# Recurrence states as 64x64 blocks per head, two chunks alternating, conditioning blocks moved behind the output norm

## The chip, the cores and the metric

The kernel runs on one core of one Trainium2 chip. The metric is the device time of one execution in microseconds (us), and a kernel's time is the median of its runs. The engines are TensorE (PE in the rows; its weight loads are PEld), VectorE (DVE), ScalarE (ACT), GpSimd (POOL) and SyncE (SP), which here only starts the loads of weights.

## The reference, cut to what matters

Two blocks of a model over 256 tokens of width 1024. The change lies in the first one, in the RWKV-7 recurrence over 8 heads of 64 and in what stands around it:

```python
mod = jax.nn.silu(c) @ cond_w + cond_b            # 6 x 1024 columns: 12 blocks of 512
shift1, scale1, gate1, shift2, scale2, gate2 = jnp.split(mod, 6, axis=-1)
...
y_conv = jax.nn.silu(layer_norm(conv(u) + conv_b, conv_ln_g, conv_ln_b))
# per token t and head: S is a 64 x 64 state
#   S_t = S_{t-1} diag(w_t) - (S_{t-1} kk_t)(kk_t * a_t)^T + v_t k_t^T ;  y_t = S_t r_t
y_rw = rwkv7_scan(rh, heads(decay), kh, vh, kk, ah)
y_rw = layer_norm(y_rw, eps=GN_EPS).reshape(bsz, seq, RW_WIDTH) * rw_lnx_g + rw_lnx_b
y_rw = (y_rw + bonus.reshape(bsz, seq, RW_WIDTH)) * g
y1 = jnp.concatenate([y_conv, y_rw], axis=-1) @ w_out
x = layer_norm(ALPHA * x + gate1[:, None, :] * y1, ln1_g, ln1_b)
```

After it come a product-key expert layer (8 heads, 16 experts a token, whose rows of 1024 floats are gathered from memory) and the second block (mixer, cross attention, feed-forward).

## The kernel before, in words

The engines run programs written out by hand, which meet in semaphores. TensorE's results go to 8 banks of PSUM; the list `JOBS` names every result in TensorE's order and the engine that takes it out, `assign_banks` deals the banks in that order, and `begin(name)` makes TensorE wait until the bank's last result has been taken out (`was_emptied`). `computed(engine, name)` is the wait the other way.

The recurrence runs in 4 chunks of 64 tokens. Tile t of 128 tokens holds chunks 2t and 2t+1, one in either half of the 128 partitions; `half_of(e)` is such a half. When the triangular inverses are done (`inv_t`, in five levels), TensorE computes:

- `wu`: per head and chunk 64 columns each of two products with the inverse, taken out by ScalarE;
- `conv_mean`, `conv_var`: the mean over channels of the convolution and of its square, by `channel_mean`; before the first it waits for the convolution's last taps (VectorE, `conv_ready`);
- `rdw`, `y_local`: what a chunk's queries read from the state before it, and from the chunk itself;
- `psi`, `phi`: what a chunk adds to the state, and the matrix by which it changes it, for a pair of heads as one 128x128 block each, of which VectorE keeps the two 64x64 diagonal blocks by a mask (L2157, L2161); it adds the decay on phi's diagonal (L2165);
- `state` 1 and 2: the state after chunks 1 and 2, each from the one before it (128x128 blocks of a head pair, L1073), and `y_state`: the states read by `rdw` (L1084);
- `y_mean`, `y_var`: mean and variance over a head's 64 channels (`over_heads`, L895), and then `out1`, the product with w_out (L1105), whose first half (of the contraction) needs the convolution's output, `y_conv_ready`, and whose second half needs the normalised recurrence, `mix_ready`.

Between these stand the conditioning vector's last blocks 8 to 11. `mod_parts(i)` (L810) multiplies silu(c) with a 1024x512 block of cond_w, which a load of 2 MB brings into one of four slots of `weight_ring`; VectorE adds bias and parts (`mod_bias`, L1973, into the single buffer `mod_sum`), `modulation(i)` (L816) sums over partitions, and ScalarE writes the result. `weight_blocks` lists the loads in order with slot and the job after which the slot is free; SyncE starts each when that job is done.

A float32 matmul has two records in the trace, one for each pass of the moving operand, so the 8 matmuls of a `by_head` half show as 16.

## Time and profile before

| | us |
|---|---|
| median of 3 runs (lowest, highest) | 1452.13 (1446.63, 1464.97) |
| profiled execution | 1464.34 |
| its span, first to last instruction | 1462.5 |
| PE / DVE / ACT / POOL busy in the span | 1168.3 / 890.2 / 507.3 / 574.2 |
| mean granted TensorE clock, share of full | 0.89 |
| first `wu` matmul, last `wu` matmul issued, first `out1` matmul | 178.8, 182.2, 234.3 |
| expert layer (gathers), about | 300 to 1073 |

The profile's times count from the span's start. An engine's busy time counts the records of its instructions; where TensorE's are short, a record covers more than the time by which the next one follows. The granted clock is a share of 2.4 GHz, and takes the two values 1 and 0.5 in this trace; a window's value is their mean.

### The profile page before, as it was taken

What the parts mean: (1) busy time and instruction counts of PE and PEld (TensorE: products, weight loads), DVE (VectorE), ACT (ScalarE), POOL (GpSimd) and SP (SyncE); (2) the same over time, 40 slices, a digit from 0 to 9 for tenths busy, and PEclk for the clock granted to TensorE, in tenths of its full rate; (3) what the DMA queues carried; (4) which work ended last, traced back from release to release, by engine and by line L of the source; (5) the groups of instructions that cost most, each with busy time, mean ns of one, the idle gap of its engine ahead of it and who ended that gap; (6) DMA issues with size and microseconds to landing.
All of it is one profiled execution on the core that took longest, in us unless ns stands there. A gap on an engine that the chain in (4) does not pass through costs nothing.

```text
span 1462.5 us, 17535 instructions
## 1 busy us (share of the span) xinstructions
PE 1168.3 (80%) x6306; PEld 769.8 (53%) x6306; DVE 890.2 (61%) x1704; ACT 507.3 (35%) x1098; POOL 574.2 (39%) x642
## 2 busy tenths in 40 slices
PE   4999989857988657587879487558749987799997
PEld 1977754744553223232354133223329966699985
DVE  3577745862545573767494585557475665488773
ACT  1564311314241322224133233123125543265551
POOL 5055300244546666576656666666610020000000
PEclk9999988978999888797879788768979998899999
DMA  9363543497989999899989999999975415256530
GB/s 355 119 237 116 176 144 112 149 355 276 334 327 386 338 378 377 334 381 335 383 306 340 350 368 365 378 335 375 365 285 194 144 34 168 72 185 193 185 137 30
DMA packets 139775, 381.11 MB, mean 261 GB/s; under 512 B 10708, under 2 KB 37743, under 8 KB 139707
## 3 DMA queue, kind: packets, MB, share of 16 engines
q0 software_dynamic: 73728, 268.47, 48.9%
q1 hardware_dynamic: 64656, 108.87, 21.7%
q10 hardware_dynamic: 1322, 2.85, 0.6%
q8 instruction: 45, 0.74, 0.2%
q14 instruction: 24, 0.19, 0.0%
HBM read 379.10 MB, written 1.05 MB: 260 GB/s over the span
## 4 chain that ended last, share of the span: by engine, by line
PE 51%; POOL 14%; issue 12%; DVE 10%; DMA 7%; ACT 3%; another core or an unknown queue 1%; DVEq 1%; ACTq 0%; SPq 0%; POOLq 0%
PE banks L1165 12%; POOL arena L731 8%; PE banks L841 7%; PE banks L843 7%; PE banks L842 7%; POOL arena L738 6%; PE banks L783 4%; PE banks L1124 3%; DMA arena<-in_peer_v,arena 3%; DMA arena<-in_peer_u,arena 3%; DVE arena L2303 2%; PE banks L955 2%; DMA weight_ring<-in_cond_w 2%; PE banks L1105 1%; PE banks L810 1%
## 5 line engine op out<-in xcount | busy, mean ns | idle before, releaser
L1165 PE MATMUL banks<-arena 128*128 128x512 f32 x1012 | 496.5, 654 | 186.3 <-issue 117.0
L1165 PEld LDWEIGHTS banks<-arena 128*128 128x128 f32 x1012 | 211.2, 212 | 468.8 <-issue 410.5
L2303 DVE SCALAR_TENSOR_TENSOR arena<-arena,banks 128x1024 f32<-128x1024 f32 x256 | 308.7, 1220 | 213.4 <-DMA arena<-in_peer_u,arena 173.1
L738 POOL DMA_INDIRECT arena<-in_peer_v,arena x256 | 243.6, 952 | 205.6 <-PE banks L1165 105.9
L731 POOL DMA_INDIRECT arena<-in_peer_u,arena x256 | 243.4, 951 | 80.7 <-issue 74.7
L843 PE MATMUL banks<-hi_h,low_slot 128*128 128x256 f32 (+2 forms) x600 | 171.4, 286 | 0.0
L1671 ACT ACTIVATE arena<-arena 128x8 f32<-128x8 f32 x32 | 6.7, 208 | 356.7 <-issue 182.8
L843 PEld LDWEIGHTS banks<-hi_h,low_slot 128*128 128x128 f32 (+2 forms) x600 | 113.0, 188 | 0.5
L841 PE MATMUL banks<-hi_h,hi_w 128*128 128x256 f32 (+1 forms) x352 | 101.3, 288 | 2.7 <-DVE lo_h L2408 2.7
L842 PE MATMUL banks<-lo_h,hi_w 128*128 128x256 f32 (+1 forms) x352 | 100.0, 284 | 0.0
L1666 ACT ACTIVATE arena<-ident,arena 128x128 f32<-128x128 f32 x256 | 78.3, 388 | 4.8 <-issue 4.2
L1677 ACT ACTIVATE arena<-arena 128x128 f32<-128x128 f32 x256 | 78.2, 388 | 3.4 <-issue 0.2
L1124 PE MATMUL banks<-hT,weight_ring 128*128 128x128 f32 (+1 forms) x384 | 62.0, 318 | 16.8 <-issue 15.2
L696 POOL TENSOR_TENSOR arena<-arena 128x512 f32<-128x512 f32 x30 | 43.0, 1434 | 74.0 <-ACT arena L1537 72.5
L841 PEld LDWEIGHTS banks<-hi_h,hi_w 128*128 128x128 f32 (+1 forms) x352 | 67.3, 191 | 3.1 <-DVE hT L2387 3.1
L1124 PEld LDWEIGHTS banks<-hT,weight_ring 128*128 128x128 f32 x384 | 56.3, 199 | 23.4 <-issue 18.3
L842 PEld LDWEIGHTS banks<-lo_h,hi_w 128*128 128x128 f32 (+1 forms) x352 | 67.3, 191 | 0.0
L2568 DVE SCALAR_TENSOR_TENSOR arena<-banks,col,arena 128x255 f32<-128x255 f32 (+3 forms) x88 | 38.4, 477 | 31.5 <-ACT arena L1906 30.8
L719 POOL COPY arena<-arena 128x16 uint32<-128x16 uint32 x16 | 3.4, 213 | 125.7 <-DVE arena L2283 125.6
L750 POOL TENSOR_TENSOR low_slot<-weight_ring,hi_out 128x4096 fp32r<-128x4096 f32 x1 | 8.9, 8903 | 109.7 <-ACT hi_out L1828 109.7
L783 PE MATMUL banks<-hT,weight_ring 128*128 128x256 f32 x192 | 49.1, 421 | 1.5 <-DVE hT L2387 0.8
L2419 DVE TENSOR_TENSOR low_slot<-weight_ring,hi_w 128x2048 fp32r<-128x2048 f32 (+1 forms) x22 | 49.2, 2242 | 1.8
(376 smaller groups left out, 1920.6 us busy)
## 6 DMA issues: line engine op xcount, KB each, us to landing
weight_ring<-in_cond_w SPq DMA_DIRECT2D x12, 2048.0 KB, 8.9
weight_ring<-in_w_in SPq DMA_DIRECT2D x11, 2048.0 KB, 9.0
weight_ring<-in_ffn_w_up SPq DMA_DIRECT2D x20, 1024.0 KB, 7.3
weight_ring<-in_ffn_w_down SPq DMA_DIRECT2D x5, 2048.0 KB, 7.8
weight_ring<-in_w_out SPq DMA_DIRECT2D x4, 2048.0 KB, 8.0
weight_ring<-in_peer_wq SPq DMA_DIRECT2D x4, 2048.0 KB, 8.0
arena<-in_peer_u,arena POOLq DMA_INDIRECT x256
arena<-in_peer_v,arena POOLq DMA_INDIRECT x256
```

The source lines that it names most:

```text
L731: g.indirect_dma_start(u_rows[:, j, :], None, A["peer_u"], bass.IndirectOffsetOnAxis(ap=row, axis=0)).then_inc(sem(f"u_in_{j}"), 16)
L738: g.indirect_dma_start(v_rows[:, j, :], None, A["peer_v"], bass.IndirectOffsetOnAxis(ap=row, axis=0)).then_inc(sem(f"v_in_{j}"), 16)
L783: last = mm(b[0:width, i * SEQ:(i + 1) * SEQ], w[:, k, f * P:f * P + width], src[:, k, :], start=(k == 0), stop=(k == KD - 1))
L841: mm(out_, sh, mh, start=first, stop=False)
L842: mm(out_, sh, ml, start=False, stop=False)
L843: return mm(out_, sl, mh, start=False, stop=last)
L1124: last = mm(b[:, half * n:half * n + n], w[:, k, f * P:f * P + P], hT[:, k, tok], start=(k == 0), stop=(k == KD - 1))
L1165: last = mm(acc[i], diag[:, r, j, :], v_rows[:, j, i * 512:(i + 1) * 512], start=False, stop=False)
L1666: fn(gate_diag[:, j, :], ident[:, :], ACT.Copy, scale=gates[:, bass.ds(n * TOPK + (8 * r + j), 1)])
L1677: ins = fn(diag[:, r, j, :], gate_diag[:, j, :], ACT.Copy, scale=gz[:, r, j:j + 1])
L2303: ins = v.scalar_tensor_tensor(out=u_rows[:, j, :], in0=u_rows[:, j, :], scalar=1.0, in1=h2_banks[t], op0=ALU.mult, op1=ALU.mult, accum_ou ...
L2419: signal(v.tensor_tensor(dst, w, hi_w[:, i % 4, :, 0:n], ALU.subtract), sem("up_split"))
```

## The change

1. `psi`, `phi` and `state` are computed per head as 64x64 blocks, two heads of a pair stacked on the two halves of the partitions; the masks go. VectorE writes decay times identity into phi early (two instructions before the convolution's taps of the first level) and later only adds phi's product.
2. Where two chunks of a tile are computed, their matmuls alternate (`state_in(0, 1)`, `read_matrix`, `own_chunk`), each chunk in its bank.
3. New order: psi, phi, states, rdw and y_local come right behind `wu`, ahead of `conv_mean`. ScalarE instead of VectorE takes psi out.
4. Conditioning blocks: `mod_parts(8)` stands behind `y_state`, `conv_var` and `y_mean` follow, `modulation(8)` stands between `y_mean` and `y_var`, and blocks 9 to 11 come behind `y_var`, ahead of `out1`. w_out's first half is loaded into the slot that block 9 leaves, ahead of the keys.
5. ScalarE takes `y_var` out ahead of the convolution's Silu; VectorE's reciprocal for `y_rs` stands behind `mod_bias(11)`.

```diff
@@ -115,19 +115,13 @@
...
+JOBS += [(("y_mean", i), "dve") for i in range(2)] + modulation_jobs(8) + [(("y_var", i), "act") for i in range(2)]
+JOBS += part_jobs(9) + part_jobs(10) + modulation_jobs(9) + part_jobs(11) + modulation_jobs(10) + modulation_jobs(11)
...
@@ -242,11 +236,11 @@
...
-              (("cond", 10), 3, ("modp", 10)), (("cond", 11), 2, ("modp", 11)), (("keys",), 1, ("keys_T", 3)),
-              (("w_out", 0), 3, ("out1", 0, 0)), (("w_out", 1), 2, ("out1", 1, 1)),
+              (("cond", 10), 3, ("modp", 10)), (("cond", 11), 2, ("modp", 11)),
+              (("w_out", 0), 1, ("out1", 0, 0)), (("keys",), 3, ("keys_T", 3)), (("w_out", 1), 2, ("out1", 1, 1)),
...
@@ -1022,56 +1016,79 @@
...
+            def state_in(*chunks):
+
+                banks = {c: begin("psi", c) for c in chunks}
+                for h in range(NHEAD):
+                    out_ = half_of(h % 2), slice(HD * (h // 2), HD * (h // 2) + HD)
+                    ch = slice(h * HD, (h + 1) * HD)
+                    for c in chunks:
+                        t, s = c // 2, half_of(c % 2)
+                        mm(banks[c][out_], kend_t[s, t, ch], v_t[s, t, ch], start=True, stop=False)
+                    for c in chunks:
+                        t, s = c // 2, half_of(c % 2)
+                        last = mm(banks[c][out_], bend_t[s, t, ch], wu[s, t, 1, h, :], start=False, stop=True)
+                        if h == NHEAD - 1:
+                            done(last)
+
+            def state_change(c):
+                b, t, s = begin("phi", c), c // 2, half_of(c % 2)
+                for h in range(NHEAD):
+                    last = mm(b[half_of(h % 2), HD * (h // 2):HD * (h // 2) + HD], wu[s, t, 0, h, :], bend_t[s, t, h * HD:(h + 1) * HD],
+                              start=True, stop=True)
+                done(last)
+
+            def read_matrix(t):
+                banks = [begin("rdw", t, e) for e in range(2)]
+                for h in range(NHEAD):
+                    for e in range(2):
+                        s = half_of(e)
+                        last = mm(banks[e][half_of(h % 2), half_of(h // 2)], wu[s, t, 0, h, :], pairs[s, t, PLACE[h], 1, :], start=True, stop=True)
+                        if h == NHEAD - 1:
+                            done(last)
+
+            def own_chunk(t):
+                banks = [begin("y_local", t, e) for e in range(2)]
+                for j in range(NPAIR):
+                    for h in (2 * j, 2 * j + 1):
+                        for e in range(2):
+                            s = half_of(e)
+                            mm(banks[e][half_of(h % 2), half_of(j)], v_t[s, t, h * HD:(h + 1) * HD], pairs[s, t, PLACE[h], 3, :],
+                               start=True, stop=False)
+                    for h in (2 * j, 2 * j + 1):
+                        for e in range(2):
+                            s = half_of(e)
+                            last = mm(banks[e][half_of(h % 2), half_of(j)], wu[s, t, 1, h, :], pairs[s, t, PLACE[h], 1, :],
+                                      start=False, stop=True)
+                            if h == NHEAD - 1:
+                                done(last)
...
                 b = begin("state", c)
                 if c == 1:
-                    pe.wait_ge(sem("phi_ready"), 2)
+                    was_emptied(pe, "psi", 0)
+                    was_emptied(pe, "phi", 1)
                 else:
                     was_emptied(pe, "state", 1)
                 src = psi[:, 0, :, :] if c == 1 else state[:, 0, :, :]
-                for j in range(NPAIR):
-                    last = mm(b[:, j * P:(j + 1) * P], phi[:, c - 1, j, :], src[:, j, :], start=True, stop=True)
+                for h in range(NHEAD):
+                    s, j = half_of(h % 2), h // 2
+                    last = mm(b[s, j * HD:(j + 1) * HD], phi[s, c - 1, j, :], src[s, j, :], start=True, stop=True)
                 done(last)
+
+            was_emptied(pe, "wu", 0, 1)
+            state_in(0, 1)
+            state_change(1)
+            read_matrix(0)
+            was_emptied(pe, "wu", 1, 1)
+            state_in(2)
+            state_change(2)
+            next_state(1)
+            read_matrix(1)
+            own_chunk(0)
+            next_state(2)
+            own_chunk(1)
+            channel_mean("conv_mean", conv, "conv_ready")
@@ -1080,16 +1097,24 @@
...
-                    for j in range(NPAIR):
-                        last = mm(b[:, j * P + half:j * P + half + CHUNK], src[:, j, :], rdw[:, t, j, half:half + CHUNK],
+                    for h in range(NHEAD):
+                        s, j = half_of(h % 2), h // 2
+                        last = mm(b[s, j * P + half:j * P + half + CHUNK], src[s, j, :], rdw[s, t, j, half:half + CHUNK],
                                   start=True, stop=True)
                 done(last)
-            mod_parts(11)
+            mod_parts(8)
+            channel_mean("conv_var", conv_t, "conv_sq_ready")
             was_emptied(pe, "y_state", 1)
             over_heads("y_mean", mean_head, y_rw)
-            modulation(11)
+            modulation(8)
             pe.wait_ge(sem("y_sq_ready"), 1)
             over_heads("y_var", mean_head, y_sq)
+            mod_parts(9)
+            mod_parts(10)
+            modulation(9)
+            mod_parts(11)
+            modulation(10)
+            modulation(11)
@@ -1597,36 +1622,43 @@
...
+            def take_psi(c):
+                computed(act, "psi", c)
+                empty(fn(psi[:, c, :, :], bank("psi", c)[:, 0:NPAIR * HD].rearrange("p (a b) -> p a b", b=HD), ACT.Copy), "psi", c)
+
+            def take_local(t):
                 for e in range(2):
                     computed(act, "y_local", t, e)
                     empty(fn(y_rw[:, :, (2 * t + e) * CHUNK:(2 * t + e + 1) * CHUNK],
                              bank("y_local", t, e)[:, 0:NPAIR * CHUNK].rearrange("p (a b) -> p a b", b=CHUNK), ACT.Copy), "y_local", t, e)
-                modulation(8 + t)
-                if t == 0:
-                    was_emptied(act, "conv_mean")
-                    signal(fn(conv_t, conv, ACT.Square), sem("conv_sq_ready"))
-                    computed(act, "conv_var")
-                    empty(fn(conv_r, bank("conv_var")[:, 0:SEQ], ACT.Sqrt, bias=eps[:, 0:1]), "conv_var")
-            modulation(10)
+
+            for c in range(NCH - 1):
+                take_psi(c)
+            act.wait_ge(sem("taps_added"), CONV_K - 1)
+            for t in range(NT):
+                take_local(t)
+            was_emptied(act, "conv_mean")
+            signal(fn(conv_t, conv, ACT.Square), sem("conv_sq_ready"))
+            computed(act, "conv_var")
+            empty(fn(conv_r, bank("conv_var")[:, 0:SEQ], ACT.Sqrt, bias=eps[:, 0:1]), "conv_var")
+            was_emptied(act, "y_mean", 1)
+            signal(fn(y_sq, y_rw, ACT.Square), sem("y_sq_ready"))
+            modulation(8)
+            for i in range(2):
+                computed(act, "y_var", i)
+                empty(fn(y_rs[:, 2 * i:2 * i + 2, :], bank("y_var", i).rearrange("p (a b) -> p a b", a=2), ACT.Sqrt,
+                         bias=eps[:, 1:2]), "y_var", i)
+            modulation(9)
...
@@ -2127,6 +2159,10 @@
...
+            was_emptied(dve, "rw_T", "bend", 1)
+            for c in (1, 2):
+                step(v.tensor_tensor(phi[:, c - 1, :, :], ident_c.unsqueeze(1).to_broadcast([P, NPAIR, HD]),
+                                     chunk_decay[:, :, c:c + 1].to_broadcast([P, NPAIR, HD]), ALU.mult))
@@ -2141,40 +2177,33 @@
...
+            def add_change(c):
+                computed(dve, "phi", c)
+                empty(v.tensor_tensor(phi[:, c - 1, :, :], phi[:, c - 1, :, :],
+                                      bank("phi", c)[:, 0:NPAIR * HD].rearrange("p (a b) -> p a b", b=HD), ALU.add), "phi", c)
+
+            def add_read(t):
                 for e in range(2):
                     computed(dve, "rdw", t, e)
                     empty(v.tensor_tensor(rdw[:, t, :, e * CHUNK:(e + 1) * CHUNK],
                                           bank("rdw", t, e)[:, 0:NPAIR * CHUNK].rearrange("p (a b) -> p a b", b=CHUNK),
                                           kr[:, :, t, 1, e * CHUNK:(e + 1) * CHUNK], ALU.add), "rdw", t, e)
...
+
+            def add_state(c):
                 computed(dve, "state", c)
-                empty(v.tensor_tensor(state[:, c - 1, :, :], bank("state", c).rearrange("p (a b) -> p a b", b=P), psi[:, c, :, :], ALU.add),
-                      "state", c)
+                was_emptied(dve, "psi", c)
+                empty(v.tensor_tensor(state[:, c - 1, :, :], bank("state", c)[:, 0:NPAIR * HD].rearrange("p (a b) -> p a b", b=HD),
+                                      psi[:, c, :, :], ALU.add), "state", c)
+
+            add_change(1)
+            add_read(0)
+            add_change(2)
+            add_state(1)
+            add_read(1)
+            add_state(2)
+            computed(dve, "conv_mean")
+            empty(v.tensor_tensor(conv, conv, bank("conv_mean")[:, 0:SEQ].unsqueeze(1).to_broadcast([P, 4, SEQ]), ALU.subtract),
+                  "conv_mean")
@@ -2182,12 +2211,17 @@
...
-            mod_bias(11)
+            mod_bias(8)
             for i in range(2):
                 computed(dve, "y_mean", i)
                 y = y_rw[:, 2 * i:2 * i + 2, :]
                 empty(v.tensor_tensor(y, y, bank("y_mean", i).rearrange("p (a b) -> p a b", a=2), ALU.subtract), "y_mean", i)
+            was_emptied(dve, "conv_var")
+            step(v.reciprocal(conv_r, conv_r))
+            settled()
+            signal(v.tensor_tensor(conv, conv, conv_r.unsqueeze(1).to_broadcast([P, 4, SEQ]), ALU.mult), sem("conv_n_ready"))
+            for i in (9, 10, 11):
+                mod_bias(i)
```

TensorE, from the last products with a mask to come to the first conditioning block, before (`L816` is modulation(8), `L1049` and `L1050` psi, `L1057` phi, `L918` conv_var, `L810` mod_parts(9)):

```order
L1049 MATMUL banks<-arena 128x128
L1050 MATMUL banks<-arena 128x128
L1057 MATMUL banks<-arena 128x128 [waits emptied_by_dve]
L1057 MATMUL banks<-arena 128x128 x3
L918 MATMUL banks<-arena,mean_all 128x256 [waits conv_sq_ready,emptied_by_dve]
L918 MATMUL banks<-arena,mean_all 128x256 x3
L810 MATMUL banks<-weight_ring,mem_kv 32x512 [waits slot_in_1,emptied_by_dve]
L810 MATMUL banks<-weight_ring,mem_kv 32x512 x7
```

The same engine now, where chunk 2's psi (L1027, L1030) ends and phi (L1037), state 1 (L1076), rdw of tile 1 (L1046) and y_local of tile 0 (L1056) follow:

```order
L1027 MATMUL banks<-arena 64x64
L1030 MATMUL banks<-arena 64x64
L1037 MATMUL banks<-arena 64x64 [waits emptied_by_act]
L1037 MATMUL banks<-arena 64x64 x7
L1076 MATMUL banks<-arena 64x64 [waits emptied_by_dve,emptied_by_act]
L1076 MATMUL banks<-arena 64x64 x7
L1046 MATMUL banks<-arena 64x64 [waits emptied_by_dve,emptied_by_act]
L1046 MATMUL banks<-arena 64x64 x15
L1056 MATMUL banks<-arena 64x64 [waits emptied_by_dve]
```

No mean, no conditioning block stands between them any more, and state 1 comes before the second tile's rdw and y_local.

TensorE from state 1 on, before (`L1073` state, `L1084` y_state, `L895` y_mean):

```order
L1073 MATMUL banks<-arena 128x128 [waits phi_ready,emptied_by_dve]
L1073 MATMUL banks<-arena 128x128 x3
L816 MATMUL banks<-mem_kv,ones 128x512 [waits emptied_by_dve]
L1073 MATMUL banks<-arena 128x128 [waits emptied_by_dve,emptied_by_act]
L1073 MATMUL banks<-arena 128x128 x3
L1084 MATMUL banks<-arena 128x64 [waits emptied_by_dve,emptied_by_act]
L1084 MATMUL banks<-arena 128x64 x3
L1084 MATMUL banks<-arena 128x64 [waits emptied_by_dve,emptied_by_act]
L1084 MATMUL banks<-arena 128x64 x7
L810 MATMUL banks<-weight_ring,mem_kv 32x512 [waits slot_in_2,emptied_by_dve]
L810 MATMUL banks<-weight_ring,mem_kv 32x512 x7
L895 MATMUL banks<-arena,mean_head 128x512 [waits emptied_by_dve] x2
```

The same engine now, from conv_mean (L912) on; `L1102` is y_state, `L804` mod_parts(8), `L889` y_mean and y_var, `L810` modulation(8):

```order
L912 MATMUL banks<-arena,mean_all 128x256 [waits taps_added,conv_ready,emptied_by_dve]
L912 MATMUL banks<-arena,mean_all 128x256 x3
L1102 MATMUL banks<-arena 64x64 [waits emptied_by_dve]
L1102 MATMUL banks<-arena 64x64 x7
L1102 MATMUL banks<-arena 64x64 [waits emptied_by_dve,emptied_by_act]
L1102 MATMUL banks<-arena 64x64 x15
L804 MATMUL banks<-weight_ring,mem_kv 32x512 [waits slot_in_2,conv_ready]
L804 MATMUL banks<-weight_ring,mem_kv 32x512 x7
L912 MATMUL banks<-arena,mean_all 128x256 [waits conv_sq_ready,emptied_by_act]
L912 MATMUL banks<-arena,mean_all 128x256 x3
L889 MATMUL banks<-arena,mean_head 128x512 [waits emptied_by_dve]
L889 MATMUL banks<-arena,mean_head 128x512 [waits emptied_by_act]
```

modulation(10) and mod_parts(11) have left the place around the states; blocks 9, 10 and 11 stand behind y_var now.

ScalarE between its last y_local (`L1604`) and y_var (`L1628`), before:

```order
L1522 ACTIVATE weight_ring<-banks,eps 128x512 [waits mm_done]
L1522 ACTIVATE weight_ring<-banks 128x512 [waits mm_done]
L1616 ACT_TABLE_LOAD
L1616 ACTIVATE hT<-arena,col 128x256 [waits conv_n_ready]
L1616 ACTIVATE hT<-arena,col 128x256 x3
L1622 DMA arena<-in_ln_g 128x1024 [waits y_conv_ready,mm_done]
L1622 DMA arena<-in_ln_b 128x1024
L1624 ACTIVATE arena<-arena 128x1024 [waits emptied_by_dve]
L1522 ACTIVATE weight_ring<-banks 128x512 [waits mm_done]
L1628 ACT_TABLE_LOAD
L1628 ACTIVATE arena<-banks,eps 128x512 [waits mm_done] x2
```

and now, from conv's square (L1641) to the last modulation (L1547):

```order
L1641 ACTIVATE arena<-arena 128x1024 [waits emptied_by_dve]
L1643 ACTIVATE arena<-banks,eps 128x256 [waits mm_done]
L1645 ACTIVATE arena<-arena 128x1024 [waits emptied_by_dve]
L1547 ACTIVATE weight_ring<-banks,eps 128x512 [waits mm_done]
L1649 ACTIVATE arena<-banks,eps 128x512 [waits mm_done] x2
L1547 ACTIVATE weight_ring<-banks,eps 128x512 [waits mm_done]
L1655 ACT_TABLE_LOAD
L1655 ACTIVATE hT<-arena,col 128x256 [waits conv_n_ready]
L1655 ACTIVATE hT<-arena,col 128x256 x3
L1659 DMA arena<-in_ln_g 128x1024 [waits y_conv_ready]
L1659 DMA arena<-in_ln_b 128x1024
L1547 ACTIVATE weight_ring<-banks 128x512 [waits mm_done] x2
```

y_var (L1649) is taken out ahead of the Silu (L1655), and the Silu, which `out1` waits for, stands behind modulation(9).

## Rows read from the trace of the kernel before

**Rows 1.** Windows of the stretch: busy us and records by engine, granted clock, DMA share.

```profile
182.50:185.90 3.40, 0.00 (x0) 0.00 (x0) 3.24 (x8) 0.60 (x1) 0.00 (x0) 0.81 0.00 0
185.90:192.40 6.50, 6.46 (x26) 3.15 (x26) 1.22 (x1) 0.00 (x0) 0.00 (x0) 0.57 0.00 0
...
212.30:216.00 3.70, 1.13 (x9) 1.00 (x9) 3.67 (x4) 0.00 (x0) 0.00 (x0) 0.91 0.67 214
216.00:228.40 12.40, 12.40 (x51) 8.28 (x51) 2.25 (x4) 3.95 (x6) 0.00 (x0) 0.50 0.45 167
...
234.30:262.00 27.70, 27.70 (x68) 12.34 (x67) 20.32 (x22) 1.68 (x4) 0.00 (x0) 1.00 0.26 91
...
300.00:1073.00 773.00, 561.34 (x1329) 268.25 (x1330) 452.80 (x1079) 227.21 (x645) 477.15 (x515) 0.85 0.94 352
```

**Rows 2.** Chain of waits, 183 to 235 us: start, us on the chain, what.

```profile
185.94 3.75 PE banks L918 x8
...
200.24 1.92 PE banks L918 x8
202.16 1.85 PE banks L810 x16
...
206.44 1.06 PE banks L816 x2
...
215.11 0.75 DVE mem_kv L1973
...
224.76 3.57 PE banks L810 x16
...
231.36 1.07 ACT arena L1624
232.47 1.98 PE banks L895 x4
```

**Rows 3.** Timeline, TensorE's matmuls: start, us, engine, line, records (x).

```profile
129.89 1.31 PE L968 MATMUL banks<-arena 64*64 64x128 f32 x38
138.27 2.08 PE L955 MATMUL banks<-arena 64*64 64x64 f32 x64
...
192.36 0.80 PE L1032 MATMUL banks<-arena 64*64 64x64 f32 x26
...
194.79 1.12 PE L816 MATMUL banks<-mem_kv,ones 128*128 128x512 f32 x2
195.85 0.49 PE L1049 MATMUL banks<-arena 64*128 64x128 f32 x2
...
199.18 1.05 PE L1057 MATMUL banks<-arena 64*128 64x128 f32 x8
...
217.84 1.91 PE L1073 MATMUL banks<-arena 128*128 128x128 f32 x8
219.54 5.22 PE L1084 MATMUL banks<-arena 128*128 128x64 f32 x24
```

**Rows 4.** Timeline, VectorE and ScalarE: start, us, engine, line; idle before in brackets.

```profile
184.97 0.87 DVE L2050 SCALAR_TENSOR_TENSOR arena<-arena,col,banks 128x256 f32<-128x256 f32 x2
...
218.69 1.28 ACT L1616 ACT_TABLE_LOAD   x1
219.99 2.07 ACT L1616 ACTIVATE hT<-arena,col 128x256 f32<-128x256 f32 x4
221.39 0.42 DVE L2183 TENSOR_TENSOR arena<-arena,banks 128x256 f32<-128x256 f32 x1 [0.91 <-PE banks L1084]
...
230.64 0.69 DVE L2190 TENSOR_TENSOR arena<-arena,banks 128x512 f32<-128x512 f32 x1 [0.17 <-PE banks L895]
...
235.51 6.55 DVE L2192 RECIPROCAL arena<-arena 128x1024 f32<-128x1024 f32 x1 [4.19 <-ACT arena L1628]
...
246.04 1.23 DVE L2202 TENSOR_TENSOR hT<-arena 128x1024 f32<-128x1024 f32 x1
```

**Rows 5.** Loads started by SyncE, 110 to 300 us: median us to landing.

```profile
weight_ring<-in_w_out SPq DMA_DIRECT2D x2, 2048.0 KB, 7.8
```

106 lines of the change are left out of this document (13 added, 93 removed).

## The prediction

> **What bounds the kernel now.** I read the windows of the stretch first, for who is busy and at what clock, then the chain of waits, then the timeline for the length of each piece. The change touches the program from the end of wu (182.5 us) to the first matmul of out1 (234.3 us), 51.8 us. TensorE sets the time there: it is busy in nearly all of it, and the chain runs through its lines [rows 1, 2]. Three things make these 51.8 us long:
>
> - Idle time. TensorE does nothing from 182.5 to 185.9, since conv_mean waits for VectorE's last taps (they end at 184.97 + 0.87 = 185.84), and works only 1.13 of the 3.7 us from 212.3 to 216.0 [rows 1, 4]. The second hole ends when VectorE, which did the reciprocal for conv and its product first, gets to the bias that modulation(10) waits for [rows 2].
> - The clock. Behind each hole the granted clock stands at 0.5, that is 1.2 instead of 2.4 GHz: it averages 0.57 from 185.9 to 192.4, and is 0.50 from 216.0 to 228.4, under full load [rows 1]. The same conv mean of 8 records takes 3.75 us there and 1.92 us at full clock; mod_parts takes 3.57 and 1.85 us [rows 2].
> - Matmuls that leave the array half empty. psi and phi use 64 of its rows, and the states and y_state multiply 128x128 blocks of which half is zero [rows 3].
>
> Behind out1 the expert layer (300 to 1073 us) keeps the DMA engines at 0.94 [rows 1]. Nothing there waits for a fixed moment: it starts when its inputs are there. A gain ahead of it should pass to the end, and a better clock inside it is not needed.
>
> **The small matmuls.** At full clock a record with 64 moving columns follows the last one by (2.08 - 0.22)/63 = 29.5 ns in the inverse levels; 0.22 is one record's own length. Those use two of the four 64x64 tiles at a time, always the diagonal ones [rows 3]. A record with 128 columns on half the rows takes (1.05 - 0.27)/7 = 111 ns (phi), and 37 such gaps take 1.04 us, 28 ns each, where a line alternates over all four tiles (L968) [rows 3]. So two tiles work at once if the columns differ, and the two row halves go side by side as well. For four tiles with 64 columns I estimate half of 29.5, 14.7 ns. Bounds: 14.7 and 29.5.
>
> - psi of chunks 0 and 1: before from 195.85 to phi's start at 199.07, 3.2 us. Now 64 records, two row halves side by side, but each head has two matmuls on one tile, so only one of its four passes hides under the next head's: 3 x 8 x 0.059 = 1.4 us. Chunk 2: 1.4 us again, on one row half; before 1.8 (16 records x 111 ns).
> - phi, twice 8 matmuls: 16 records x 29.5 ns = 0.47 us each, before 0.9 each.
> - rdw and y_local of a tile: before 2.43 us from 192.36 to 194.79 [rows 3]. Now 96 records x 14.7 ns = 1.4 us.
> - state, twice: 16 records x 29.5 ns = 0.47 us, before 1.05 at full clock (it shows 1.91 at half) [rows 3].
> - y_state: 48 records x 29.5 ns = 1.4 us, before 5.22 at half clock, so 2.6 at full.
>
> Together 8.9 us of work, before 16.4 at full clock: 7.5 us less.
>
> A rule speaks against part of this: the half-size blocks of the two heads in state and y_state go into one bank, from two row halves. The inverse levels do just that (each half's result in its half of one bank) and show 29.5 ns [rows 3]. By the Trainium skill (TensorEngine Tiling (Array Packing), Gotcha 1: PSUM Pressure) different row tiles cannot access the same PSUM bank simultaneously; taken strictly, state and y_state would take twice their 2.3 us. By this rule, the trace does not agree, and the sum goes by the row.
>
> **The new schedule.** I lay it out from 182.5 us with durations at full clock.
>
> - TensorE goes on at once: the chain from psi to y_local is 7.5 us without y_state and ends at 190.0. Its first need of VectorE is phi 1 for state 1, at 186.7; VectorE leaves the taps at 185.84 and needs 0.42 for a 256-column addition [rows 4], so 186.3: no wait. rdw, phi 2 and state 1 follow there (0.75, 0.42, 0.42 us), in time for y_local and state 2. ScalarE takes psi beside it.
> - conv_mean 1.92, y_state 1.4, mod_parts(8) 1.85, conv_var 1.92, y_mean 1.98: 199.1. mod_parts(8) covers VectorE's 1.2 us on conv, its y_state additions and ScalarE's square.
> - modulation(8) 1.06: 200.2. It covers most of VectorE's last subtraction (0.69) and ScalarE's square (1.07 [rows 2]), which end at 201.1: 0.9 us of wait remain. y_var 1.98: 203.1.
> - mod_parts(9) and (10), 3.7: 206.8; modulation(9) 1.06: 207.9; mod_parts(11) 1.85: 209.7; modulation(10): 210.8. mod_sum is one buffer, so bias 11 (0.75 [rows 2]) can only follow: wait 0.85, modulation(11) ends at 212.7.
> - The Silu on ScalarE is queued behind modulation(9): 0.6 to take it out, 1.28 for its table and 2.07 for the Silu [rows 4]: 211.9, just hidden. This wait is new; behind it stand only the ln1 loads and later modulations.
> - w_out's first half is loaded into block 9's slot, so the load starts at 203.1 + 1.85 + 0.1 = 205.1 and lands 7.8 us later [rows 5] at 212.9. That is the last to come: out1 starts at **212.9**.
>
> Block 11's load starts when block 8 is used (195.3) and, at the same 7.8 us, is there at 203.1, long before 207.9. The keys now follow w_out's first half in SyncE's queue, and w_out's second half starts at 209.8; both have the 13.8 us of out1's first half, plus, for VectorE, the long reciprocal: bias 11 at 211.6, then the 11.8 us from 235.51 to 247.27 [rows 4] give mix_ready at 223.4, before 226.7. The cover is 3.3 us thin. The two early instructions for phi (at most 0.42 each) lie on VectorE ahead of a 3.3 us idle stretch and cost nothing; at worst 0.8.
>
> So out1 starts 234.3 - 212.9 = **21.4 us** earlier. The same from the other side: 9.0 us by the clock (half of the 12.4 us at 0.50, and 0.43 of the 6.5 us at 0.57), 5 us of idle time (7 before, 2 left) and 7.5 us of smaller matmuls make 21.5. The profiled execution took 1464.34 us (span 1462.5), 12 us over the median; 21.4 off each give 1442.9 and, for the median, 1452.1 - 21.4 = **1430.7**, say 1431.
>
> **Rivals.**
>
> - The clock falls again. The new stretch has short matmuls only from 182.5 to 190, and small waits at 200 and 211. For it: the low clock of 216.0 to 228.4 lasted through y_state's short records [rows 1, 3]. Against it: a hole of over 2 us stood before each low stretch, and the inverse levels' 64-column records ran at full clock. Price: a low stretch of 12.4 us costs half, 6.2: 1437. Chance 0.18.
> - The four tiles don't keep up. If alternating row halves brings nothing over 29.5 ns, rdw and y_local take 2.8 us a tile and psi 0 and 1 twice 1.4: + 2 x 1.4 + 1.4 = 4.2: 1435. A milder case is a floor on how closely matmuls follow each other. The closest in these rows is 28 ns; with that, the 192 records of rdw and y_local cost 2.6 more and psi 0 and 1 0.4: 1434. Chance 0.10 for both. The Trainium skill (TensorE: Matmul & The Clock Gate, Back-to-back issue gap) gives such a floor of about 25 ns for up to 64 columns. By this figure the two would cost 2.2 us more, an estimate from it; the rows at 28 ns agree with it so far.
> - A load is late. w_out's first half shares the engines with the keys and the second half. If the keys' 1 MB get in first, half of its 7.8 us for 2 MB, + 3.9: 1435. Chance 0.07.
> - Slower than before. If every change of tile drained the array, each record would pay the 111 ns of the wide ones: the 400 records from psi to y_state would take 44.4 us instead of 8.9, + 35.5, and out1 would start at 248.4: 1466, and with the clock at half in it 1500 and more. It decides from (8.9 + 21.4)/400 = 76 ns a record. The 28 ns of L968, which changes tile with each matmul, speaks against it. Chance 0.03.
> - The change doesn't do what it says: VectorE still ends the taps at 185.84, and if the order of additions behind them held TensorE, the gain would lack some 3 us: 1434. Chance 0.05.
>
> **How the numbers follow.** The forecast, 1431, has the rest, 0.57. The cases down to 3 in 100 lie between 1431 and 1437. The runs of one kernel spread from 1447 to 1465, so a median of three can be off by some 7 us either way, and a sum that misses gains (a shorter y_mean, less idle time) could be low by 3. That gives 1419 to 1445. A measurement tells about 2% from no change, here 29 us, so 1423.1 is the line: the forecast misses it by 8, which scatter and a low sum can bridge, 0.15. Slower by over 2% (1481) needs the draining case at half clock, 0.01. Within 2%: 0.84.
>
> **What would show it.** In the profile after: out1's first record comes 34 us behind wu's start, where it was 55.5 before; each us more than 34 is a us less of gain. No hole above 1.2 us in TensorE between wu and out1, and granted clock 1 throughout; rdw and y_local of a tile some 1.4 us, y_state 1.4; the last wait ahead of out1 on the load of w_out or on modulation(11). The expert layer should last as long as before. I am wrong if the clock is 0.5 anywhere in the stretch, if records of alternating halves follow at 29 ns or more, or if mix_ready comes behind out1's first half.

## The result and the profile after

| | before | after |
|---|---|---|
| median (lowest, highest), 20 runs each | 1459.42 us (1446.63, 1465.38) | 1444.74 us (1440.96, 1455.07) |
| ratio, 95% interval | | 0.9913 (0.9896, 0.9930) |
| profiled execution's span | 1462.5 us | 1453.0 us |
| first `out1` matmul, and behind wu's first | 234.3, 55.5 us | 216.0, 37.0 us |

By the ratio the gain is 12.7 us of 1459 (10 to 15); the two medians lie 14.7 us apart. The forecast was 21.4 us of gain and a time of 1431 us. Of the 14.0 us between 1430.7 and 1444.74, 7.3 come from the base: the kernel before takes 1459.42 us as a median of 20 runs, and 1452.13 was the median of three. The other 6.7 are gain that did not come. In the profile out1 starts 18.3 us earlier, so most of the schedule came as laid out, and yet the kernel gained less than that.

Windows of the profile after; the columns are those of [rows 1].

```profile
182.50:190.00 7.50, 6.67 (x330) 6.32 (x324) 6.24 (x16) 2.30 (x6) 0.00 (x0) 1.00 0.02 4
190.00:192.20 2.20, 0.65 (x29) 0.55 (x28) 0.00 (x0) 0.00 (x0) 0.00 (x0) 1.00 0.00 0
192.20:213.00 20.80, 19.41 (x145) 8.53 (x142) 9.08 (x11) 8.42 (x13) 0.00 (x0) 1.00 0.52 185
213.00:216.00 3.00, 1.10 (x2) 0.30 (x2) 3.00 (x2) 2.06 (x5) 0.00 (x0) 1.00 1.10 341
216.00:220.00 4.00, 3.96 (x6) 1.77 (x7) 3.96 (x2) 1.14 (x1) 0.00 (x0) 0.57 1.10 353
220.00:246.00 26.00, 26.00 (x67) 11.84 (x66) 14.17 (x21) 0.70 (x3) 0.00 (x0) 1.00 0.44 164
```

Against [rows 1] the two stretches at 0.57 and 0.50 are gone: the granted clock is 1.00 from wu to out1. A short one at 0.57 now lies at out1's start. Timeline of TensorE after:

```profile
186.52 0.59 PE L1076 MATMUL banks<-arena 64*64 64x64 f32 x13 [0.62 <-DVE arena L2182]
...
191.59 0.27 PE L1056 MATMUL banks<-arena 64*64 64x64 f32 x2 [1.55 <-issue]
...
192.20 1.99 PE L912 MATMUL banks<-arena,mean_all 128*128 128x256 f32 x8
194.12 1.61 PE L1102 MATMUL banks<-arena 64*64 64x64 f32 x48
...
203.10 1.98 PE L889 MATMUL banks<-arena,mean_head 128*128 128x512 f32 x4 [1.01 <-ACT arena L1645]
205.01 3.64 PE L804 MATMUL banks<-weight_ring,mem_kv 128*32 128x512 f32 x32
...
213.55 1.10 PE L810 MATMUL banks<-mem_kv,ones 128*128 128x512 f32 x2 [0.93 <-DVE mem_kv L2005]
216.04 2.05 PE L1130 MATMUL banks<-weight_ring,hT 128*128 128x512 f32 x2 [1.39 <-issue]
```

L1102 is y_state: 48 records in 1.61 us, where [rows 3] had 24 wide ones in 5.22. Of the waits, 1.01 (square, forecast 0.9) and 0.93 (bias 11, forecast 0.85) came as said. Three had not been forecast: 0.62 us for VectorE's phi 1 ahead of state 1, a stop of 1.55 us in the middle of y_local of tile 1, and 1.39 us ahead of out1, which ends when w_out's first half has landed (requested at 207.00 instead of 205.1, and 9.0 us under way instead of 7.8). A small stop of 0.21 us in rdw of tile 1 came with them.

A fourth lies ahead of wu, where the prediction saw no cost. VectorE, then TensorE, after:

```profile
133.98 2.92 DVE L2164 TENSOR_TENSOR arena<-masks,st 128x256 f32<-128x256 f32 x2
136.94 2.71 DVE L2082 SCALAR_TENSOR_TENSOR banks<-arena,col,banks 128x256 f32<-128x256 f32 x6
139.56 0.74 DVE L2005 SCALAR_TENSOR_TENSOR mem_kv<-arena,ident,banks 128x512 f32<-128x512 f32 x1
```

```profile
140.44 1.10 PE L810 MATMUL banks<-mem_kv,ones 128*128 128x512 f32 x2 [1.31 <-DVE mem_kv L2005]
```

The same place before (`L1973` is that bias, `L816` TensorE's use of it, `L2139` VectorE's next addition):

```profile
138.47 0.75 DVE L1973 SCALAR_TENSOR_TENSOR mem_kv<-arena,ident,banks 128x512 f32<-128x512 f32 x1 [0.45 <-PE banks L810]
142.53 0.69 DVE L2139 TENSOR_TENSOR arena<-arena,banks 128x512 f32<-128x512 f32 x1 [3.31 <-PE banks L955]
```

```profile
140.28 1.12 PE L816 MATMUL banks<-mem_kv,ones 128*128 128x512 f32 x2
```

The two early instructions for phi take 1.46 us each, not 0.42. The idle stretch of 3.3 us that the prediction counted on lies behind the bias of conditioning block 4; ahead of it VectorE had 0.45 us to spare, and the bias was ready 1.06 us before TensorE took it. So 2.92 us do not fit, the bias comes late, and TensorE waits 1.31 us for it. The profiles of the other kernels that keep these lines in place show the same 1.31 or 1.32.

### The profile page after: what moved, and what is told of

It reads as the page before. It is cut to its first block, busy times and chain, and to the rows that moved or that the text cites. A ratio compares the mean times of both kernels' runs of the same rounds, so it can differ in the third digit from the quotient of the medians.

```text
span 1453.0 us, 17742 instructions
## 1 busy us (share of the span) xinstructions
PE 1155.9 (80%) x6410; PEld 758.1 (52%) x6410; DVE 886.9 (61%) x1695; ACT 508.3 (35%) x1101; POOL 574.3 (40%) x642
## 4 chain that ended last, share of the span: by engine, by line
PE 46%; POOL 17%; issue 16%; DVE 9%; DMA 5%; ACT 4%; another core or an unknown queue 2%; DVEq 1%; ACTq 0%; SPq 0%; POOLq 0%
PE banks L1190 9%; POOL arena L725 9%; POOL arena L732 8%; PE banks L835 7%; PE banks L837 7%; PE banks L836 7%; PE banks L777 3%; PE banks L1149 2%; DMA arena<-in_peer_v,arena 2%; PE banks L949 2%; PE banks L1130 2%; DMA weight_ring<-in_cond_w 2%; DVE arena L2337 2%; PE banks L804 1%
```

## The experiments

The runs were made on several chips. On some both kernels take about 90 us less than on the others (1365 against 1455 us), because the expert layer's gathers run with fewer stops there; a comparison is always with the kernel before on the same chip. "wu to out1" is the time from wu's first matmul to out1's first.

**Both kernels again.** No edit.

> The changed kernel, unedited, once more. Its first profile gave back part of its lead in the expert layer: 16 us ahead up to the 55th of the 512 gathers, 11 behind the 57th, 9.5 at the end. If that is a property of the program (theory A: a fetch of ScalarE's instructions falls under the expert loads), this run's profile loses some 5 us at the same gather and ends about 10 us under the kernel before (ratio 0.991). If it is scatter (theory B), the loss is at another gather or absent, and the span varies by several us while the time from wu to out1 stays at 37.0 us.

> The kernel before, unedited, so that a profile of it stands beside the others of the same chip: in the four runs so far the expert layer's 512 gathers paced at 1.25 us each, with fewer long stops than in the first two profiles. Theory A (the lead is given back in the expert layer): the time from the first to the last gather is here some 5 to 8 us shorter than the 682 to 690 us of the changed kernels. Theory B (scatter of both ends): it is 682 to 690 us here as well, and the lead at the last gather equals the lead at out1's end to within the scatter of one execution, 3 to 4 us. In both, out1 starts 55.5 us behind wu's start.

> The changed kernel once more, beside it. wu to out1 35 to 37 us (the two profiles so far: 37.0 and 35.2), with the stop of 1.0 to 1.6 us inside y_local of tile 1 again if it belongs to the program (a fetch of TensorE's instructions), gone if it is scatter. Theory A: its gathers take 5 to 8 us longer than those of the kernel before in the same call. Theory B: the same to within 4 us. Ratio 0.991 in both.

The ratios of the changed kernel were 0.9909 (0.9880 to 0.9938) and 0.9914 (0.9880 to 0.9948), of the kernel before against itself 1.0028 (0.9996 to 1.0061). Wu to out1 was 35.2 and 34.6 us after. The surprise was the kernel before: 48.5 us, not 55.5. Its windows, and timeline of TensorE:

```profile
184.00:192.50 8.50, 6.47 (x72) 3.71 (x74) 3.95 (x8) 0.00 (x0) 0.00 (x0) 0.80 0.00 0
216.00:228.40 12.40, 11.36 (x62) 6.50 (x61) 3.92 (x6) 7.93 (x11) 0.00 (x0) 1.00 0.76 278
```

```profile
186.03 3.31 PE L918 MATMUL banks<-arena,mean_all 128*128 128x256 f32 x8 [3.47 <-issue]
...
215.04 1.10 PE L816 MATMUL banks<-mem_kv,ones 128*128 128x512 f32 x2 [2.45 <-DVE mem_kv L1973]
...
216.87 3.01 PE L1084 MATMUL banks<-arena 128*128 128x64 f32 x24
```

The same program, the same holes of 3.47 and 2.45 us, but behind the second one the clock stays at 1.00 and y_state takes 3.01 instead of 5.22 us. So single executions of both kernels were profiled again.

> The kernel before again, for its clock between wu and out1. Of its two profiles one has 0.50 from 216.0 to 228.4 us and takes 55.5 us from wu's start to out1, the other runs there at full clock and takes 48.5. Theory: the low clock behind the idle time is there in some executions only; the typical one has little of it, so that the 9.0 us that the prediction counted as gain are mostly no property of the program. This profile then shows 48 to 50 us (or 55 once more). Rival: the 48.5 was the exception; then 54 to 56 us here and in the next.

> The same once more: theory 48 to 50 us from wu's start to out1 in at least one of the two, rival 54 to 56 in both.

> The changed kernel again, beside them: 34.5 to 37 us from wu's start to out1, at full clock until out1 starts, and in the middle of y_local of tile 1 TensorE stops for 0.5 to 1.6 us, as in the three profiles before. The difference to the kernel before at out1's start is by the theory 11 to 15 us where that one has no low clock there.

> The kernel before once more: by the theory one of its two forms, 48 to 50 us from wu's start to out1, or 55.5 with the half clock from about 216 to 228; the five profiles together then have it in two or three. Rival: something between, 51 to 54 us, which would mean that there are not two forms but a spread.

> The kernel before, for the count alone: 48 to 50 us from wu's start to out1 if the usual form is the one at full clock, 55.5 us with 0.50 from about 216 to 228 otherwise. Rival: a time between the two, 51 to 54 us.

> The same once more. If both this and the last show 55.5 us, the low clock is there in four of seven, and the missing gain needs another cause than the clock.

| | wu to out1, us | mean |
|---|---|---|
| before, seven profiles | 55.5, 48.5, 49.7, 55.6, 48.6, 51.0, 50.9 | 51.4 |
| after, four profiles | 37.0, 35.2, 34.6, 36.2 | 35.7 |

Behind the second hole the granted clock is 0.50 for 13 us in two profiles (55.5 and 55.6), for some 3 us in three (49.7, 51.0, 50.9), and not at all in two (48.5, 48.6). Behind the first hole it is at 0.50 in all seven, until 3 to 6 us after the hole's end. So the expectation of two forms fell. The last profile's windows:

```profile
184.00:192.50 8.50, 5.79 (x20) 3.12 (x24) 3.75 (x7) 0.05 (x1) 0.00 (x0) 0.60 0.00 0
216.00:228.40 12.40, 10.82 (x56) 6.42 (x56) 5.24 (x9) 4.74 (x7) 0.00 (x0) 0.86 0.67 235
```

With the clock at full throughout, wu to out1 would be 46.9 us before: in the 48.5 us profile only conv_mean (3.23 us to the next piece instead of 1.92) and mod_parts(8) (2.15 instead of 1.86) still ran slow. So the low clock costs 1.6 to 8.7 us an execution, 4.5 on average; the seven scatter by 3.0 us (standard deviation), so that this average is itself known only to 1 us or so. The profile that the forecast rested on has nearly the most.

Does the expert layer give some of the lead back? From its first gather to its last, on the slower chips: before 783, 776, 791, 777 us, after 791, 776; on the faster ones before 682, 688, 689, after 690, 688. The means after are 1.7 and 2.9 us longer, but the executions of one kernel differ by 7 to 15 us. A give-back of 5 to 8 us, as feared in the expectations, would be hard to fit with this; one of 2 us is neither shown nor excluded.

**The holes alone**, in the kernel before.

```diff
@@ JOBS
-JOBS += [(("conv_mean",), "dve")] + part_jobs(8)
+JOBS += part_jobs(8) + [(("conv_mean",), "dve")]
@@ TensorE, and likewise mod_bias(8) on VectorE
-            channel_mean("conv_mean", conv, "conv_ready")
             mod_parts(8)
+            channel_mean("conv_mean", conv, "conv_ready")
@@ VectorE, in the loop over t
-                if t:
-                    was_emptied(dve, "conv_var")
-                    step(v.reciprocal(conv_r, conv_r))
...
@@ VectorE, behind the additions to state 1 and 2
+            was_emptied(dve, "conv_var")
+            step(v.reciprocal(conv_r, conv_r))
...
```

> The kernel before, with only its two holes filled: block 8's matmuls ahead of the conv mean, and VectorE's reciprocal and product for conv behind the additions to the states. Theory: that is worth the idle time that it removes, 1.9 and 2.4 us: 44 to 45 us from wu's start to out1 at full clock, ratio 0.997. Rival: the holes bring the low clock in nearly every execution, and a kernel without them gains the clock's 7 to 9 us as well: ratio 0.991 to 0.993, like the whole change. Other rival: the waits go on to the next step (the Silu or the square): 47 us or more, ratio 1.000.

> The kernel before with only its second hole filled (reciprocal and product behind the additions to the states), the first one left. Theory: the half clock of 12 us comes, where it comes, from the second hole: it is absent here, only the stretch behind the first hole shows 0.5 to 0.9, and out1 starts 44 to 46 us behind wu's start, ratio 0.994 to 0.996. Rival: the first hole's low clock brings the second stretch too; then this kernel shows half clock behind 212 us as well.

The first has both edits, the second only that of the reciprocal. TensorE with both holes filled:

```profile
187.52 1.96 PE L918 MATMUL banks<-arena,mean_all 128*128 128x256 f32 x8 [1.61 <-issue]
...
210.43 1.02 PE L816 MATMUL banks<-mem_kv,ones 128*128 128x512 f32 x2
...
222.90 13.47 PE L1105 MATMUL banks<-weight_ring,hT 128*128 128x512 f32 x31
```

and with the second alone:

```profile
187.01 3.75 PE L918 MATMUL banks<-arena,mean_all 128*128 128x256 f32 x8 [3.47 <-issue]
...
216.64 3.01 PE L1084 MATMUL banks<-arena 128*128 128x64 f32 x24
...
227.10 9.18 PE L1105 MATMUL banks<-weight_ring,hT 128*128 128x512 f32 x21
```

With both, wu to out1 is 42.6 us, which is 46.9 - 1.9 - 2.4, the clock is full from wu to out1, and the ratio is 0.9935 (0.9911 to 0.9959): 8.9 us (6 to 12), against 4.3 us of idle time plus 4.5 us of clock, 8.8. That lies between the theory (0.997, idle time alone, which is just outside the interval) and the first rival (0.991 to 0.993): the clock comes back too, by its average and not by 7 to 9 us. The close agreement of 8.9 and 8.8 is luck in view of the interval. With the second hole alone filled wu to out1 is 47.3 us, not 44 to 46, since the clock is low for 6 us behind the first hole and conv_mean still takes 3.75 us; the half clock behind the second is gone, as expected. The ratio is 0.9979 (0.9958 to 1.0001), weaker than the 0.994 to 0.996 expected. Between wu and out1 low clock was seen only where a hole had been. It is one profile each, so "never without a hole" is not shown; how long the low clock lasts behind a hole varied between executions of one program.

**The wide blocks**, in the new order.

```diff
-        phi = at(T0 + 6656, 2, NPAIR, HD)
-        psi = at(T0 + 7168, 3, NPAIR, HD)
+        phi = at(T0 + 6144, 2, NPAIR, P)
+        psi = at(T0 + 7168, 3, NPAIR, P)
-                for h in range(NHEAD):
+                for j in range(NPAIR):
...
+            mask_in(0)
+            mask_in(1)
```

The loops over pairs of heads are those of psi, phi, state and y_state; `mask_in` is VectorE's product of psi with the mask, and phi gets mask and four additions again. The two early instructions for phi are gone in this kernel, and with them TensorE's wait of 1.31 us ahead of wu.

> The new order, but psi, phi and the states as 128x128 blocks with masks and the eight scalar additions on VectorE, as in the kernel before. Theory: 5 us more of TensorE (psi 0 and 1 2.4, psi 2 1.8, phi 0.9 each, states 1.0 each, y_state 2.6 us), and VectorE's masks (0.69 each) and phi additions (1.14 each) just beside them: out1 5 to 7 us later than 37.0 behind wu's start, ratio 0.995 to 0.996. Rival: VectorE becomes the bound of the recurrence (9 us of work behind the last taps): 8 us or more, with waits for it in front of the states. Other rival: the order alone is worth all; then under 2 us.

TensorE, then VectorE:

```profile
192.17 1.13 PE L1076 MATMUL banks<-arena 128*128 128x128 f32 x8 [0.95 <-DVE arena L2196]
...
196.15 2.79 PE L1101 MATMUL banks<-arena 128*128 128x64 f32 x24
```

```profile
185.33 1.29 DVE L2174 TENSOR_TENSOR arena<-banks,same_head 128x512 f32<-128x512 f32 x2
...
190.28 1.14 DVE L2183 SCALAR_TENSOR_TENSOR arena<-ident,st,arena 128x128 f32<-128x128 f32 x4
```

Wu to out1 is 39.7 us against 35.2 of the changed kernel on the same chip, 4.5 us more; the ratio is 0.9934 (0.9909 to 0.9960) against 0.9909. That is just under the 5 to 7 expected. In the ratio the small blocks are worth some 3 us: the 4.5 less the 1.3 that they cost ahead of wu, though the two intervals overlap. VectorE holds TensorE 0.95 us at state 2 and is not the bound.

**The chunks one after the other.**

```diff
-                for j in range(NPAIR):
-                    for h in (2 * j, 2 * j + 1):
-                        for e in range(2):
+                for e in range(2):
+                    b, s = begin("y_local", t, e), half_of(e)
+                    for j in range(NPAIR):
+                        for h in (2 * j, 2 * j + 1):
```

> The chunks of a tile one after the other instead of alternating (psi, rdw and y_local). Theory: alternation puts the two row halves side by side, 14.6 ns a record against 29.5 ns, so that rdw and y_local of a tile take 2.8 us again instead of 1.4, psi 0 and 1 together 2.2 instead of 1.1: out1 starts 3.5 to 4 us later behind wu's start (37.0 now), ratio to the kernel before 0.994. Rival: what TensorE gains there it waits for VectorE and the w_out load anyway; then out1 starts less than 1.5 us later.

The end of y_local in this kernel, and y_local of tile 0 in the changed one:

```profile
197.48 0.33 PE L1053 MATMUL banks<-arena 64*64 64x64 f32 x4
197.60 0.33 PE L1050 MATMUL banks<-arena 64*64 64x64 f32 x4
```

```profile
188.13 0.33 PE L1056 MATMUL banks<-arena 64*64 64x64 f32 x8
188.25 0.33 PE L1061 MATMUL banks<-arena 64*64 64x64 f32 x8
```

Four records in 0.12 us against eight: 29 ns and 14.6 ns a record. So four tiles do work at once. But wu to out1 is 36.0 us, only 0.8 more than 35.2, and the ratio, 0.9907 (0.9878 to 0.9936), is the same. The rival held: conv_mean starts just 1.2 us later. The pieces themselves cost some 2.4 us more, not the 3.9 expected, among other things since rdw's records follow at 21 to 23 ns here and not at 29.5. The wait for VectorE ahead of state 1 (0.62) and half of the stop in y_local (1.00, here 0.49) take up some 1.2 of that, and the shorter wait for w_out (0.52, here 0.14) takes up 0.4.

**The conditioning blocks between the pieces**, as before the change (8 and 9 ahead of and behind psi and rdw, 10 and 11 between y_local and y_state).

```diff
-            mod_parts(9)
-            mod_parts(10)
-            modulation(9)
-            mod_parts(11)
-            modulation(10)
-            modulation(11)
@@ ahead of state_in(0, 1), and 9 and 10 likewise
+            mod_parts(8)
@@ behind y_state
+            mod_parts(11)
```

> Conditioning blocks 8 to 11 back between the pieces of the recurrence, with the 64x64 blocks, the alternating chunks and the early w_out kept. Theory: TensorE has the same work, so it must pay the waits of the norms (square to y_var 2 us, the Silu) without cover, but w_out's first half is there early: out1 starts 36 to 38 us behind wu's start, held by the Silu, ratio 0.991 to 0.993. Rival: VectorE, which then has the biases among the recurrence's additions, holds the states up: 39 us or more, ratio 0.994 or more. Other rival: moving the blocks is worth nothing, 34 to 35 us.

```profile
212.12 1.98 PE L889 MATMUL banks<-arena,mean_head 128*128 128x512 f32 x4 [1.01 <-ACT arena L1649]
218.27 2.08 PE L1130 MATMUL banks<-weight_ring,hT 128*128 128x512 f32 x2 [4.17 <-ACT hT L1658]
```

38.3 us against 34.6 on the same chip, ratio 0.9950 (0.9920 to 0.9980) against 0.9914. Without the blocks behind y_var, TensorE waits 4.17 us for the Silu. Moving them is worth 3.7 us between wu and out1. The ratio fits the rival's 0.994 or more, but its cause does not: no wait for VectorE in the recurrence is longer than 0.2 us. Part of it is that the clock fell to 0.50 for 3 us behind the wait of 4.17, so that out1 took 29.2 us and not 27.7.

**The last waits ahead of out1.** Block 9's matmuls ahead of y_var; and, in a kernel of its own, the keys' load behind both halves of w_out.

```diff
+            mod_parts(9)
             pe.wait_ge(sem("y_sq_ready"), 1)
             over_heads("y_var", mean_head, y_sq)
-            mod_parts(9)
@@ in the other kernel, the list of loads
-              (("w_out", 0), 1, ("out1", 0, 0)), (("keys",), 3, ("keys_T", 3)), (("w_out", 1), 2, ("out1", 1, 1)),
+              (("w_out", 0), 1, ("out1", 0, 0)), (("w_out", 1), 2, ("out1", 1, 1)), (("keys",), 3, ("keys_T", 3)),
```

> Conditioning block 9's matmuls moved ahead of y_var, into the wait for the square; w_out's first half, which takes block 9's slot, is so requested 4 us earlier. Theory: the 1.0 us wait for the square and the 1.39 us wait for w_out go, and out1 starts at 34.8 us behind wu's start instead of 37.0, held by the Silu. If the half-clock stretch inside out1 (1.75 us) came from that wait, out1 takes 27.6 us again instead of 29.4, and the lead at out1's end is 20 us instead of 16.5. Rival: the load takes the 9 us and more wherever it starts, since block 11, the keys and the second half share the engines: out1 starts at 36 or later, and the low clock stays.

> The keys' load moved behind both halves of w_out. Theory: the keys' load, requested 1.6 us behind w_out's first half, makes that half late; without it the half lands within 7.8 us instead of 9.0, and TensorE's last wait ahead of out1 (1.39 and 0.52 us in the two profiles) is gone or under 0.3 us: out1 starts 34.7 to 35.7 us behind wu's start. Rival: the load's length comes from elsewhere (how fast this chip moves data, block 11): the wait stays within 0.3 us of that of the unedited kernel in the same call. By either the ratio changes by less than 0.001.

With block 9 early, out1 follows the last modulation at once, at 33.7 us, and the ratio is 0.9896 (0.9865 to 0.9928). The theory had the Silu hold it at 34.8 us, and it did not. The load took 9.5 us, as the rival had it, but as it started early it landed 0.1 us ahead of out1. With the keys last, SyncE's loads and out1's start are:

```profile
205.84 5.00 SPq L599 DMA_DIRECT2D weight_ring<-in_w_out  x2
210.88 8.95 SPq L599 DMA_DIRECT2D weight_ring<-in_peer_k  x2
```

```profile
214.61 1.96 PE L1130 MATMUL banks<-weight_ring,hT 128*128 128x512 f32 x4 [1.11 <-issue]
```

The half is still 8.7 us under way, in the range of the unedited kernel (7.8 to 9.0), so my theory that the keys delay it fell. The rival's number fell as well: TensorE waits 1.11 us, and 0.23 in the unedited kernel of the same chip. What sets the load's length stays open. The ratio is 0.9918 (0.9889 to 0.9948), as good as unchanged. The low clock at out1's start was absent in the three other profiles of the unedited kernel, wait or not, so this wait doesn't bring it by itself.

**The two early instructions for phi** behind the bias of block 4, and then together with block 9 early.

```diff
-            was_emptied(dve, "rw_T", "bend", 1)
-            for c in (1, 2):
-                step(v.tensor_tensor(phi[:, c - 1, :, :], ...
             convolve(3)
             mod_bias(MOD_BESIDE[2])
+            was_emptied(dve, "rw_T", "bend", 1)
+            for c in (1, 2):
+                step(v.tensor_tensor(phi[:, c - 1, :, :], ...
```

> The two early instructions for phi behind the bias of conditioning block 4 instead of ahead of it, in VectorE's idle stretch of 2.4 us. Theory: TensorE's wait of 1.31 us for that bias goes, the two take 2.92 us there and delay the first inverse addition by 0.5 us at most: 0.8 to 1.3 us of gain, ratio 0.990. Rival: they are long only beside GpSimd's products, and take 0.8 us elsewhere. Other rival: the idle stretch is too short, and the inverse levels lose what the block gains: ratio unchanged, 0.991.

> The changed kernel with both moves: the early instructions for phi behind the bias, and block 9's matmuls ahead of y_var. Theory: the two gains add up, 1 us ahead of wu and 2 us behind it: 33.7 us from wu's start to out1, ratio 0.988 to 0.989. Rival: the scatter of one execution hides it, ratio 0.990 or more.

VectorE, then TensorE, of the first:

```profile
136.84 2.67 DVE L2166 TENSOR_TENSOR arena<-masks,st 128x256 f32<-128x256 f32 x2
```

```profile
137.98 1.13 PE L810 MATMUL banks<-mem_kv,ones 128*128 128x512 f32 x2
```

The wait of 1.31 us is gone, the two still take 2.67 us, and wu starts at 176.2 us; in the four profiles of the changed kernel it starts at 177.7 to 182.7. The ratio is 0.9904 (0.9881 to 0.9927).

This does not settle why they are long. The rival, that they are so only beside GpSimd's products, was not put to the test: GpSimd runs products in the new place too (from 136.55 to 139.23). The traces point its way. GpSimd from 133 us on in the changed kernel, with the two beside it, and the same three products here, where the two come later:

```profile
133.42 4.62 POOL L703 TENSOR_TENSOR arena<-arena,masks 128x512 f32<-128x512 f32 x3 [2.18 <-DVE arena L2159]
```

```profile
132.34 4.26 POOL L703 TENSOR_TENSOR arena<-arena,masks 128x512 f32<-128x512 f32 x3 [2.06 <-DVE arena L2159]
```

The last two of the three take 1.46 and 1.45 us beside them and 1.28 each without. So GpSimd at least is held up while they run. Whether they are held up by it in turn, and how long they take with GpSimd idle, no run shows.

Both moves together give 34.0 us from wu to out1 and the shortest span of that chip, 1342.7 us, but a ratio of 0.9909 (0.9888 to 0.9929), as the rival had it: 1 to 3 us is what these runs cannot tell from the change itself.

## Why the prediction was wrong

**The step that failed** is the clock's term of the sum, "9.0 us by the clock", and the step that carried it from the profile to the median: "21.4 off each". It had priced the clock from one execution alone and then took it off the median too. The seven profiles show the clock costing 1.6 to 8.7 us in the kernel before, 4.5 on average. The price in this one execution was right (8.7), its frequency was not asked. The "12 us over the median" could have been the warning. Over the median of 20 runs it is 4.9 us, about the 4.5 by which the term was too large; the other 7 us are the median of three being low, which the prediction's range had allowed for ("some 7 us either way").

The rest, by the prediction's own steps:

- Idle time and smaller matmuls, 12.4 us: 46.9 - 35.7 = 11.2 measured. Right, with some luck: psi, conv_var, y_mean and two mod_parts took together 1.3 us less than laid out, which made up for part of the waits that had not been foreseen. In detail: rdw and y_local of a tile 1.4 us (0.47 + 0.93), as forecast; psi 0 and 1 1.1 (forecast 1.4), psi 2 0.9 (1.4), phi and state 0.47 each, y_state 1.54 (1.4). That the chain ended at 192.2 instead of 190.0 comes from the wait for VectorE (0.62) and the stops (1.55 and 0.21), less the shorter psi (0.8); from one record's start to the next the three cost 0.81, 1.74 and 0.40, since a record's own 0.22 comes on top.
- VectorE "needs 0.42 ... no wait": its own times were right (185.04 + 0.87, then 0.42), but TensorE was there sooner than forecast.
- The early instructions for phi "cost nothing; at worst 0.8": wrong by size, 2.92 us, and by place: the 3.3 us idle stretch lies behind the bias and not ahead of it. Price 1.3 us in the trace, which moving them removed; the ratios cannot tell it.
- The load of w_out: 3.1 us late in the first profile, 0.2 to 1.4 us of wait in all. The rival "a load is late" came true in a small way. It was too dear at 3.9 us, and its cause, the keys, was not borne out.
- "The four tiles don't keep up": no; 14.6 ns a record, at the lower bound. The rival rested on a misread row: "the closest in these rows is 28 ns", but rdw before, 26 records in 0.80 us [rows 3], follow at (0.80 - 0.22)/25 = 23 ns, and rdw and y_local took 2.43 us a tile, not 2.8. The Trainium skill (TensorE: Matmul & The Clock Gate, Back-to-back issue gap) gives a floor of about 25 ns for up to 64 columns; over four tiles the trace does not agree. By the Trainium skill (TensorEngine Tiling (Array Packing), Gotcha 1: PSUM Pressure) different row tiles cannot access the same PSUM bank simultaneously. The trace does not agree: y_state's 48 records, from two row halves into one bank, follow each other at 29.7 ns, as those of the inverse levels do.
- The clock does not fall between wu and out1: right in all profiles after.
- "A gain ahead of it should pass to the end": the first gather starts at 264.2 us on average after (four profiles) and at 279.2 before (seven), 15.0 us apart. The runs show 12.7 us (10 to 15), so most or all of it passes on.

The account: 4.5 (clock) + 11.2 (idle time and matmuls) - 1.3 (phi) = 14.4 us, within the measured 10 to 15. The 1.7 us down to 12.7 are not accounted for; the intervals are too wide for it. The 7.0 us missing from 21.4 are 4.5 of clock (9.0 against 4.5), 1.2 of unforeseen waits and 1.3 of phi. What is open is the stop in y_local. It is in every profile of the changed kernel, 0.5 to 1.6 us long, and the kernel before has such stops in the inverse levels. Only instruction loads stand near it in the DMA view; that they cause it is argued, not shown. Also open is a stop of ScalarE: it took out scores(4) late in both profiles of the changed kernel on the slower chips (and in the kernel with the blocks between),

```profile
371.50 0.60 ACT L1447 ACTIVATE arena<-banks 128x512 f32<-128x512 f32 x1 [3.42 <-remote]
```

and did not with the keys last, nor on the faster chips. It costs some 3 to 5 us at the gather behind it, the 56th; the duration of all gathers scatters too much to show whether that lasts to the end.

## What to carry to other kernels

Price idle time and the clock behind it separately, and take the clock's price from several executions: the first is a property of the program, the second varies from run to run. The two profiles with the most low clock lie 4.9 and 7.5 us above the median of their chip, so a profile that lies above the median is a poor base for the clock's price. And take the median itself from more than three runs: here that was half of the miss in the time. Filling TensorE's two holes alone brought 8.9 us (6 to 12), the whole change 12.7 (10 to 15), and the holes are a small part of the edit. A new instruction, even a small one off the critical engine, has to be priced from a row with the same operands and the same neighbours (here two broadcast inputs, beside GpSimd's products), its place found on the right side of the idle stretch, and what is queued behind it named.

## What the hardware showed unexpectedly

- Matmuls of 64x64 on all four quarters of the array follow each other at 14.6 ns a record, on two at 21 to 30 ns (rdw 21 to 23, y_local with its chunks one after the other 29, y_state 29.7).
- Behind the same hole of 2.45 us the granted clock was 0.5 for 13 us, for some 3 us, or 1.00, in executions of one program.
- A VectorE product of 128x256 with both inputs broadcast, beside GpSimd's products, took 1.34 to 1.46 us; an addition of the same size took 0.42. GpSimd's products beside it took 1.45 instead of 1.28.
- Chips differ by 90 us in 1450 on the same kernel, nearly all in the gathers.
